# Rotary turns of twelve query tiles: block transfers and a column of signs for products with a constant matrix

## The chip, the cores and the metric

One core of one Trainium2 chip runs the whole program once. The metric is the device time of one execution in microseconds, as the median of several runs.

## The reference, cut to what matters

The model is two blocks one after the other on 512 tokens of width 1024, all float32. The first block (convolution branch, spatial gating, mixture of experts) and the feed-forward parts of the second are not touched. The part that matters is the mixing part of the second block:

```python
p = h @ w_in[l]                                  # 512 x 2416
qa, ka, va, qi, ki, wi, cq, ckv, kr = jnp.split(p, split_points, axis=-1)
qa = apply_rope(qa.reshape(B, T, 8, 64), cos_a, sin_a)     # attention queries
ka = apply_rope(ka, cos_a, sin_a)
qi = apply_rope(qi.reshape(B, T, 16, 64), cos_i, sin_i)    # index queries
ki = apply_rope(ki, cos_i, sin_i)
out_a = dsa_sparse_attention(qa, ka, va, qi, ki, wi)       # top 128 keys by index score
out_b = mla_attention(cq, ckv, kr, g_q_lat[l], g_kv_lat[l], w_uq[l], w_ukv[l], cos_b, sin_b)

def apply_rope(x, cos, sin):
    x1, x2 = jnp.split(x, 2, axis=-1)
    return jnp.concatenate([x1 * cos - x2 * sin, x1 * sin + x2 * cos], axis=-1)
```

## The kernel before

The program is written engine by engine, each with its own queue of instructions and explicit semaphores. Activations lie transposed: features on the 128 partitions, the 512 tokens along the free axis. A tile of queries is 128 x 512 and holds two heads of 64 features. The stage that the change touches is `pe_mix`, `act_mix`, `dve_mix`, `pool_mix` and `sp_mix`.

The projection `h @ w_in` runs as 20 chunks of weights in 5 groups of 4 chunks. For each chunk SyncE loads 512 KB, ScalarE writes the high half (`split_hi`, L551), VectorE the low half (`split_lo`, L556), and TensorE makes 24 products of 128x512 in three terms (L561 to L563). After four chunks VectorE reads the four banks of the group (`read_group`, L3028). Group 0 holds the keys and the narrow columns, groups 1 and 2 the eight tiles of index queries (`qi`, ropes 2 to 9), group 3 the latents, and group 4 the four tiles of attention queries (`qa`, ropes 10 to 13).

A rotation of a tile x is x * cos + R x * sin, where R is a constant 128x128 matrix that exchanges the halves of each head and negates one of them. TensorE makes R x as one float32 product of 128x512 (`rotate_rows`, L2791; the trace shows two passes for each product), GpSimd makes x * cos (L3240 for ropes 0 to 9, L3256 for 10 to 13), VectorE makes R x * sin out of PSUM (`sine`, L3045; `sines_of_queries`, L3063), and VectorE (L3053) or GpSimd (L3260) adds the two. TensorE's `rotate_rows` stands after chunk 4 (ropes 0 and 1), chunk 8 (ropes 2 to 5), chunk 12 (ropes 6 to 9), and, for ropes 10 to 13, between the K and V products of the latents (L2858, L2864) behind the last chunk.

The index products (`index_pair`, L2809) follow chunks 9, 10, 13 and 14 and read the rotated tiles; ScalarE takes their positive part, and VectorE accumulates the scores (`accumulate`, L3084). From chunk 15 on VectorE selects the top 128 keys by rounds of L3100 and L3103, in `choose_to` steps that are woven into its other work: 30 steps by the end of chunk 19, 38 before `sines_of_queries`, 70 after it, and then the rotation of the latent queries (L3162, L3166) with six more steps. When L3166 has summed a half, SyncE copies it by four DMAs (L2728) into the place from which the first scores of the attention are made (L2747). `hold_clock` (L426) makes products that nothing reads, to keep TensorE busy.

GpSimd's queue also carries `term_step` (L2260): DMAs of 704 KB each that prepare weight sums in DRAM for a later stage. 7 stand before its rotations, 7 behind the cosine of rope 5, 8 behind that of rope 9, 5 behind the latent squares.

Of the kernel before, what the change touches and what calls it, by code (L numbers as in the profile page):

```python
# [52 lines left out]
ALU = mybir.AluOpType  # L53
# [50 lines left out]
K_HALF = 1220  # L104
K_CA = 1224
# [7 lines left out]
def constants():  # L113
# [21 lines left out]
    c[:, K_HALF] = p // CAP  # L135

# [16 lines left out]
def program(nc, A, out):  # L153
    with ExitStack() as ctx:
# [2482 lines left out]
        sine_of_query = [after_groups[:, 3584 + T * i:4096 + T * i] for i in range(4)]  # L2637

# [4 lines left out]
        rot_bank = [4, 5] + [0, 1, 2, 3] + [4, 5, 6, 7] + [4, 5, 6, 7]  # L2643
# [140 lines left out]
        def pe_mix(pe):  # L2784
# [14 lines left out]
            def index_pair(p):  # L2799
                q, b = idx_pairs[p]  # L2800
                S = P * (b + 1)
                if b == 3:
                    pe.wait_ge(mx["rope"], R_QI + q + 1)
                    pe.wait_ge(mx["rot_read"], R_QI + (4 if q < 4 else 8))
# [20 lines left out]
            for c in range(4, 4 * N_MIX):  # L2825
# [15 lines left out]
                if c == 8:  # L2841
                    rotate_rows(range(2, 6))
                if c == 12:
                    rotate_rows(range(6, 10))
# [15 lines left out]
            rotate_rows(range(R_QA, len(ropes)))  # L2860
# [7 lines left out]
            pe.wait_ge(mx["rot_read"], len(ropes))  # L2868
# [41 lines left out]
        def act_mix(act):  # L2910
# [43 lines left out]
            for c in range(4, 20):  # L2954
                if c + 2 < 20:
                    mix_hi(c + 2)
                else:
                    split_hi(act, C_MO, c - 18)
# [9 lines left out]

            act.wait_ge(mx["acc"], 2 * N_IDX)
# [52 lines left out]
        def dve_mix(dve):  # L3022
# [16 lines left out]
            split_lo(dve, C_MIX, 5)  # L3039
            def sine(r):  # L3040
                kind = ropes[r][1]
                dve.wait_ge(mx["rot"], r + 1)
                if r >= 3:
                    dve.wait_ge(mx["rope"], r - 2)
                dve.tensor_tensor(pr[:, r % 3, :], psum[:, rot_bank[r], :], sin_of[kind], ALU.mult).then_inc(  # L3045
                    mx["rot_read"], 1)

            def rotated(r):
# [3 lines left out]
                if r:  # L3052
                    dve.tensor_tensor(src, cos_at(r), pr[:, r % 3, :], ALU.add).then_inc(mx["rope"], 1)  # L3053
                    return
# [5 lines left out]
            def sines_of_queries():  # L3060
                for r in range(R_QA, len(ropes)):
                    dve.wait_ge(mx["rot"], r + 1)
                    dve.tensor_tensor(sine_of_query[r - R_QA], psum[:, rot_bank[r], :], sin_of["A"], ALU.mult).then_inc(  # L3063
                        mx["rot_read"], 1)
# [67 lines left out]
            for c in range(3, 20):  # L3132
# [5 lines left out]
                if c % 4 == 3:  # L3138
                    read_group(c // 4)
# [85 lines left out]
        def pool_mix(pool):  # L3225
# [28 lines left out]
            for r in range(R_QA, len(ropes)):  # L3254
                pool.wait_ge(mx["rot"], r + 1)
# [137 lines left out]
```

## Time and profile before

| | |
|---|---|
| Median of 3 runs | 1966.82 us (1966.52 to 1968.87) |
| The profiled execution | 1966.62 us |
| Its span in the trace | 1964.6 us, 26526 instructions |
| TensorE busy | 1880.4 us (96%) |
| VectorE, ScalarE, GpSimd busy | 1110.6, 673.7 and 354.2 us (57%, 34%, 18%) |
| Granted TensorE clock, mean | 0.997 |

The mixing stage up to the start of its attention lies at about 1305 to 1489 us of the span. Rows of the page and of the trace have times in us from the start of the span. A group of instructions is named by its line, engine, operation, tile written <- tiles read, sizes and count.

### The profile page before, as it was taken

What the parts mean: (1) busy time and instruction counts of PE and PEld (TensorE: products, weight loads), DVE (VectorE), ACT (ScalarE), POOL (GpSimd) and SP (SyncE); (2) the same over time, 40 slices, a digit from 0 to 9 for tenths busy, and PEclk for the clock granted to TensorE, in tenths of its full rate; (3) what the DMA queues carried; (4) which work ended last, traced back from release to release, by engine and by line L of the source; (5) the groups of instructions that cost most, each with busy time, mean ns of one, the idle gap of its engine ahead of it and who ended that gap; (6) DMA issues with size and microseconds to landing.
All of it is one profiled execution on the core that took longest, in us unless ns stands there. A gap on an engine that the chain in (4) does not pass through costs nothing. (4 is left out here: it accounts for less than half of the span.)

```text
span 1964.6 us, 26526 instructions
## 1 busy us (share of the span) xinstructions
PE 1880.4 (96%) x9569; PEld 1343.8 (68%) x9570; DVE 1110.6 (57%) x1680; ACT 673.7 (34%) x1030; POOL 354.2 (18%) x430
## 2 busy tenths in 40 slices
PE   8999999998997789998899999999999899999998
PEld 7888888785332233333588887887665589999886
DVE  4998993444111111111634336965687638777897
ACT  4234435432000000000422224562336746444566
POOL 2023233201221112222011000012255500010100
PEclk9999999999999999999999999999999999999999
DMA  6489999997999999999466534677980065666565
GB/s 208 149 291 291 252 326 237 301 381 290 424 426 427 426 427 425 393 426 423 163 214 214 155 96 140 193 181 184 234 192 12 1 148 155 181 181 183 174 197 171
DMA packets 202680, 485.84 MB, mean 247 GB/s; under 512 B 34892, under 2 KB 113153, under 8 KB 177370
## 3 DMA queue, kind: packets, MB, share of 16 engines
q1 hardware_dynamic: 171802, 384.24, 54.5%
q0 software_dynamic: 30768, 100.31, 20.0%
q8 instruction: 62, 1.02, 0.2%
q14 instruction: 32, 0.26, 0.0%
q10 hardware_dynamic: 16, 0.00, 0.0%
HBM read 475.17 MB, written 111.67 MB: 299 GB/s over the span
## 5 line engine op out<-in xcount | busy, mean ns | idle before, releaser
L561 PE MATMUL psum<-h_hi,w_hi 128*128 128x512 f32 (+1 forms) x1240 | 449.8, 363 | 6.2 <-DVE h_lo L1043 1.9
L563 PE MATMUL psum<-h_hi,w_lo 128*128 128x512 f32 (+1 forms) x1240 | 445.3, 359 | 0.0
L562 PE MATMUL psum<-h_lo,w_hi 128*128 128x512 f32 (+1 forms) x1240 | 445.1, 359 | 0.0
L556 DVE TENSOR_TENSOR w_lo<-w_raw,w_hi 128x1024 fp32r<-128x1024 f32 (+1 forms) x144 | 178.2, 1238 | 296.3 <-ACT w_hi L551 296.2
L551 ACT ACTIVATE w_hi<-w_raw 128x1024 fp32r<-128x1024 f32 (+1 forms) x144 | 151.7, 1053 | 502.0 <-PE psum L563 454.3
L561 PEld LDWEIGHTS psum<-h_hi,w_hi 128*128 128x128 f32 x1240 | 234.2, 189 | 46.0 <-issue 7.1
L562 PEld LDWEIGHTS psum<-h_lo,w_hi 128*128 128x128 f32 x1240 | 234.3, 189 | 35.3 <-issue 1.4
L563 PEld LDWEIGHTS psum<-h_hi,w_lo 128*128 128x128 f32 x1240 | 234.2, 189 | 34.9
L1409 PE MATMUL psum<-arena,w_raw 128*64 128x512 f32 x800 | 181.7, 596 | 13.5 <-DMA arena<-in_w_expert_up_dram 12.6
L1544 ACT ACTIVATE w_raw<-psum 128x256 f32<-128x256 f32 x36 | 13.8, 384 | 464.1 <-PE psum L1409 464.1
L1071 DVE SCALAR_TENSOR_TENSOR arena<-arena,vec 128x512 f32<-128x512 f32 x240 | 162.6, 748 | 1.0 <-ACT arena L898 1.0
L1409 PEld LDWEIGHTS psum<-arena,w_raw 128*64 128x64 f32 x800 | 54.5, 137 | 118.1 <-issue 95.7
L2044 ACT ACTIVATE w_hi<-w_raw 128x1024 fp32r<-128x1024 f32 x77 | 81.7, 1061 | 115.9 <-PE psum L563 114.8
L2092 DVE TENSOR_TENSOR w_lo<-w_raw,w_hi 128x1024 fp32r<-128x1024 f32 x77 | 95.6, 1242 | 43.5 <-ACT w_hi L2044 43.4
L1419 PE MATMUL psum<-arena,w_raw 128*64 128x512 f32 x400 | 93.0, 608 | 12.7 <-DMA arena<-in_w_expert_down_dram 11.7
L1788 POOL DMA_INDIRECT expert_rows<-w_raw,scatter_now x34 | 35.1, 1032 | 330.8 <-DVE w_raw L1713 322.1
L1702 DVE TENSOR_TENSOR w_raw<-w_raw,psum 128x256 f32<-128x256 f32 x36 | 15.2, 421 | 138.2 <-ACT w_raw L1544 138.2
L2260 POOL DMA_DIRECT2D weight_terms<-in_w_down_dram x72 | 58.8, 896 | 188.8 <-DMA weight_terms<-in_w_down_dram 108.0
L1713 DVE TENSOR_SCALAR w_raw<-psum,arena 128x512 f32<-128x512 f32 x34 | 25.5, 751 | 118.3 <-PE psum L1419 118.3
L2346 PE MATMUL psum<-w_hi,down_operands 128*128 128x512 f32 x224 | 87.7, 391 | 1.9 <-DVE down_operands L2587 1.9
L2348 PE MATMUL psum<-w_lo,down_operands 128*128 128x512 f32 x224 | 87.2, 389 | 0.0
L2347 PE MATMUL psum<-w_hi,down_operands 128*128 128x512 f32 x224 | 87.2, 389 | 0.0
(394 smaller groups left out, 3197.8 us busy)
## 6 DMA issues: line engine op xcount, KB each, us to landing
arena<-in_w_expert_gate_dram SPq DMA_DIRECT2D x44, 1024.0 KB, 19.4
arena<-in_w_expert_up_dram SPq DMA_DIRECT2D x44, 1024.0 KB, 23.4
arena<-in_w_expert_down_dram SPq DMA_DIRECT2D x22, 2048.0 KB, 28.8
weight_terms<-in_w_down_dram POOLq DMA_DIRECT2D x60, 512.0 KB, 7.9
w_raw<-in_w_in_dram SPq DMA_DIRECT2D x44, 512.0 KB, 8.6
expert_down_third<-in_w_expert_down_dram SPq DMA_DIRECT2D x10, 2048.0 KB
expert_input<-in_w_expert_gate_dram SPq DMA_DIRECT2D x20, 1024.0 KB, 22.4
expert_input<-in_w_expert_up_dram SPq DMA_DIRECT2D x20, 1024.0 KB, 26.3
```

The lines of the kernel that those rows point to most:

```text
L551: eng.activation(whi[:, (c0 + k) % SPLIT, :, 0:n], raw[:, slot, :, 0:n], ACT.Copy).then_inc(w_hi, 1)
L556: eng.tensor_tensor(wlo[:, s, :, 0:n], raw[:, slot, :, 0:n], whi[:, s, :, 0:n].bitcast(F32), ALU.subtract).then_inc(w_lo, 1)
L561: eng.matmul(o, w_h, x_h, start=first, stop=False)
L562: eng.matmul(o, w_h, x_l, start=False, stop=False)
L563: return eng.matmul(o, w_l, x_h, start=False, stop=last)
L1071: dve.scalar_tensor_tensor(out=conv[:, c, :], in0=a_pad[:, c, j:j + T], scalar=conv_w[:, c, j:j + 1], in1=conv[:, c, :], op0=ALU.mult, op1 ...
L1409: mm = pe.matmul(psum[q * CAP:(q + 1) * CAP, 2 + b, :].rearrange("p (w n) -> p w n", w=2), xgT[b][:, k % 4, (k // 4) * CAP:(k // 4 + 1) * ...
L1419: mm = pe.matmul(psum[q * CAP:(q + 1) * CAP, 6 + b, :], heT[b][:, k % 2, (k // 2) * CAP:(k // 2 + 1) * CAP], wd[w][:, k, q * T:(q + 1) * T ...
L2092: dve.tensor_tensor(wlo4[:, r % SPLIT], raw4[:, r % RAW], whi4[:, r % SPLIT].bitcast(F32), ALU.subtract).then_inc(w_lo, 1)
L2346: pe.matmul(o, x_h[:, a, f], w_h[:, a, :], start=begin, stop=False)
L2347: pe.matmul(o, x_l[:, a, f], w_h[:, a, :], start=False, stop=False)
L2348: mm = pe.matmul(o, x_h[:, a, f], w_l[:, a, :], start=False, stop=end)
```

## The change

For the eight index tiles and the four attention tiles the product with R is gone. ScalarE issues four DMAs for each group of four tiles (`turn_rows`), which copy blocks of 32 partitions x 2048 floats from the tiles to another place with neighbouring blocks exchanged: 0 with 1, 2 with 3. The sign of R becomes a column of constants (`K_SIGN`, -1 or 1 by partition), and VectorE makes (copy * sign) * sin in one `scalar_tensor_tensor` (`signed_sine`), in place, from two SBUF tiles. Groups 1 and 2 use the place of the attention queries (`ar3[:, 0:2048]`), which the last group read fills later; group 4 uses the place where the four sines stood before. Ropes 0 and 1 stay as they were. TensorE no longer waits for the sines to be read before its index products and before the latent queries' products; it waits for the last group read instead.

```diff
+K_SIGN = 1221
+    c[:, K_SIGN] = np.where(p % HDA < HDA // 2, -1, 1)
+        turned_keys = [qa[:, i, :] for i in range(4)]
+        rows_at = [ar3[:, 18688:20736], ar3[:, 20736:22784], ar3[:, 0:2048]]
+        turn_in = x_in[0:3]
+
+        def turn_rows(act_eng, i):
+
+            group_read(act_eng, G_MIX + (1, 2, 4)[i])
+            if i == 1:
+                act_eng.wait_ge(mx["rope"], R_QI + 4)
+            to, source = rows_at[2] if i < 2 else after_groups[:, 3584:5632], rows_at[i]
+            for b in (32, 0, 96, 64):
+                act_eng.dma_start(to[b:b + 32], source[b ^ 32:(b ^ 32) + 32]).then_inc(turn_in[i], 16)
...
-                    pe.wait_ge(mx["rot_read"], R_QI + (4 if q < 4 else 8))
...
-                if c == 8:
-                    rotate_rows(range(2, 6))
-                if c == 12:
-                    rotate_rows(range(6, 10))
...
-            rotate_rows(range(R_QA, len(ropes)))
...
-            pe.wait_ge(mx["rot_read"], len(ropes))
+            group_read(pe, G_MIX + 4)
...
             for c in range(4, 20):
+                if c in (8, 12):
+                    turn_rows(act, c // 4 - 2)
                 if c + 2 < 20:
                     mix_hi(c + 2)
...
+            turn_rows(act, 2)
             act.wait_ge(mx["acc"], 2 * N_IDX)
...
+            def signed_sine(r, part):
+                dve.wait_ge(turn_in[(r - R_QI) // 4], 80)
+                dve.scalar_tensor_tensor(out=part, in0=part, scalar=sign, in1=sin_of["A"], op0=ALU.mult,
+                                         op1=ALU.mult).then_inc(mx["rot_read"], 1)
+
             def sine(r):
                 kind = ropes[r][1]
+                if r >= R_QI:
+                    signed_sine(r, turned_keys[(r - R_QI) % 4])
+                    return
...
-                    dve.tensor_tensor(src, cos_at(r), pr[:, r % 3, :], ALU.add).then_inc(mx["rope"], 1)
+                    part = turned_keys[(r - R_QI) % 4] if r >= R_QI else pr[:, r % 3, :]
+                    dve.tensor_tensor(src, cos_at(r), part, ALU.add).then_inc(mx["rope"], 1)
...
             def sines_of_queries():
                 for r in range(R_QA, len(ropes)):
-                    dve.wait_ge(mx["rot"], r + 1)
-                    dve.tensor_tensor(sine_of_query[r - R_QA], psum[:, rot_bank[r], :], sin_of["A"], ALU.mult).then_inc(
-                        mx["rot_read"], 1)
+                    signed_sine(r, sine_of_query[r - R_QA])
...
                 if c % 4 == 3:
+                    if c == 19:
+                        dve.wait_ge(mx["rope"], R_QA)
                     read_group(c // 4)
...
             for r in range(R_QA, len(ropes)):
-                pool.wait_ge(mx["rot"], r + 1)
+                pool.wait_ge(turn_in[2], 80)
                 pool.tensor_tensor(cos_at(r), ropes[r][0], cos_of[ropes[r][1]], ALU.mult).then_inc(mx["cos"], 1)
```

The semaphores `turn_in` are at 16 from the loads of x at the start, so 80 means that all four transfers of a group have landed.

## Rows read from the trace of the kernel before

**Rows 1.** The page, part 1: busy time, share of the span and instructions of each engine.

```profile
PE 1880.4 (96%) x9569; PEld 1343.8 (68%) x9570; DVE 1110.6 (57%) x1680; ACT 673.7 (34%) x1030; POOL 354.2 (18%) x430
```

**Rows 2.** Timeline of TensorE, two stretches: start, us, line, tiles, count.

```profile
1356.96 3.60 PE L2791 MATMUL psum<-arena,const 128*128 128x512 f32 x8
...
1360.63 0.39 PE L562 MATMUL psum<-h_lo,w_hi 128*128 128x512 f32 x1
...
1365.97 1.45 PE L2809 MATMUL psum<-arena 64*128 64x512 f32 x6
...
1394.60 3.60 PE L2791 MATMUL psum<-arena,const 128*128 128x512 f32 x8
```

**Rows 3.** The same before the attention, with idle time and its releaser.

```profile
1462.41 7.03 PE L2864 MATMUL psum<-arena 128*128 128x512 f32 x16
...
1486.44 1.46 PE L426 MATMUL psum<-const 128*128 128x256 f32 x6
1489.15 0.68 PE L2747 MATMUL psum<-arena 96*128 96x128 f32 x4 [1.25 <-DMA arena<-expert_input]
```

**Rows 4.** Stretches: each engine's busy us, clock, DMA share, GB/s.

```profile
1460.00:1480.00 20.00, 20.00 (x47) 8.77 (x47) 20.00 (x59) 5.15 (x9) 11.19 (x9) 1.00 0.18 62
```

**Rows 5.** Timeline of VectorE, 1454 to 1485.

```profile
1454.99 2.28 DVE L3028 TENSOR_TENSOR arena<-psum,stat_std 128x2048 f32<-128x2048 f32 x1
...
1463.91 2.46 DVE L3063 TENSOR_TENSOR expert_input<-psum,const 128x512 f32<-128x512 f32 x4
...
1484.20 0.67 DVE L3166 TENSOR_TENSOR expert_input<-expert_input 128x512 f32<-128x512 f32 x1
```

**Rows 6.** One line, SyncE's DMAs of 64 KB: duration of issue, then landing.

```profile
L2728 SPq DMA_DIRECT2D arena<-expert_input x8: 588/591/740, 1484.9 to 1489.5; - x8
...
DMA to landing us min/median/max: 2.0/2.0/2.3
```

**Rows 7.** DMA issues at 1342, 1400 and 1340 to 1500: KB each, us to landing.

```profile
w_raw<-in_w_in_dram SPq DMA_DIRECT2D x1, 512.0 KB, 3.5
...
w_raw<-in_w_in_dram SPq DMA_DIRECT2D x3, 512.0 KB, 5.7
...
up_terms<-up_terms POOLq DMA_DIRECT2D x11, 704.0 KB, 14.0
```

**Rows 8.** Stretches where the transfers will fall, columns as in rows 4.

```profile
1356.00:1359.00 3.00, 3.00 (x10) 1.71 (x10) 0.98 (x2) 1.06 (x1) 2.63 (x3) 1.00 0.34 118
1393.00:1396.00 3.00, 3.00 (x12) 1.99 (x11) 0.98 (x2) 1.06 (x1) 1.97 (x2) 1.00 0.81 159
...
1458.00:1461.00 3.00, 3.00 (x8) 1.33 (x7) 3.00 (x11) 1.83 (x4) 0.85 (x1) 1.00 0.99 251
```

**Rows 9.** Timeline of VectorE around the rotations of groups 1 and 2.

```profile
1354.01 2.28 DVE L3028 TENSOR_TENSOR arena<-psum,stat_std 128x2048 f32<-128x2048 f32 x1
1358.31 1.65 DVE L556 TENSOR_TENSOR w_lo<-w_raw,w_hi 128x1024 fp32r<-128x1024 f32 x1 [2.02 <-ACT w_hi L551]
...
1362.28 1.46 DVE L3053 TENSOR_TENSOR arena<-arena 128x512 f32<-128x512 f32 x1
...
1391.67 2.28 DVE L3028 TENSOR_TENSOR arena<-psum,stat_std 128x2048 f32<-128x2048 f32 x1
```

**Rows 10.** The page, part 5: a group of instructions of the first block.

```profile
L1071 DVE SCALAR_TENSOR_TENSOR arena<-arena,vec 128x512 f32<-128x512 f32 x240 | 162.6, 748 | 1.0 <-ACT arena L898 1.0
```

**Rows 11.** Timeline of GpSimd at groups 1 and 3.

```profile
1356.37 4.74 POOL L3240 TENSOR_TENSOR arena<-arena,const 128x512 f32<-128x512 f32 x3 [22.00 <-DVE arena L3028]
1361.90 1.29 POOL L3240 TENSOR_TENSOR arena<-arena,const 128x512 f32<-128x512 f32 x1 [0.80 <-DVE arena L3053]
...
1460.15 4.96 POOL L3256 TENSOR_TENSOR arena<-arena,const 128x512 f32<-128x512 f32 x4 [2.93 <-PE psum L2791]
```

**Rows 12.** Stretches in the expert stage, columns as in rows 4.

```profile
700.00:706.00 6.00, 2.13 (x14) 0.78 (x11) 1.02 (x2) 0.38 (x1) 0.00 (x0) 0.99 1.02 428
706.00:710.00 4.00, 4.00 (x14) 1.25 (x12) 0.00 (x0) 0.00 (x0) 0.00 (x0) 0.59 1.01 426
```

More of the change, by code:

```diff
@@ L2642, in program @@
         pe_rows = slice(NOPE, HQ)
-        rot_bank = [4, 5] + [0, 1, 2, 3] + [4, 5, 6, 7] + [4, 5, 6, 7]
+        rot_bank = [4, 5]
         rot_group = [0] * 2 + [1] * 4 + [2] * 4 + [4] * 4
@@ L3039, in dve_mix @@
             split_lo(dve, C_MIX, 5)
+            sign = const[:, K_SIGN:K_SIGN + 1]
+            def signed_sine(r, part):
+                dve.wait_ge(turn_in[(r - R_QI) // 4], 80)
+                dve.scalar_tensor_tensor(out=part, in0=part, scalar=sign, in1=sin_of["A"], op0=ALU.mult,
+                                         op1=ALU.mult).then_inc(mx["rot_read"], 1)
             def sine(r):
                 kind = ropes[r][1]
+                if r >= R_QI:
+                    signed_sine(r, turned_keys[(r - R_QI) % 4])
+                    return
                 dve.wait_ge(mx["rot"], r + 1)
-                if r >= 3:
-                    dve.wait_ge(mx["rope"], r - 2)
                 dve.tensor_tensor(pr[:, r % 3, :], psum[:, rot_bank[r], :], sin_of[kind], ALU.mult).then_inc(
```

## The prediction

> **What bounds the kernel now.** I read the page first: TensorE is busy 96% of 1964.6 us [rows 1], and the granted clock is 1.00 in every stretch of this stage that I quote [rows 4, 8]. That average says nothing of the stage in question, so I went on to the timelines of 1350 to 1490 us, engine by engine. The twelve rotations removed are three groups of four, and the groups don't have the same bound.
>
> Groups 1 and 2 (eight index-query tiles) stand in TensorE's stream without a gap on either side [rows 2]. VectorE and ScalarE idle there, waiting for TensorE. What TensorE saves is saved, if nothing new makes it wait. Group 3 (four attention-query tiles) also stands in a full TensorE stream [rows 3], but there VectorE is busy 20.00 of 20.00 us [rows 4], TensorE ends first and then idles 1.25 us for a DMA [rows 3]. That DMA (eight copies of the rotated latent queries) is released by VectorE's L3166, at the end of its unbroken chain: group read, sines, selection steps, L3162, L3166 [rows 5]. So before the attention stage VectorE is the bound, and time saved on TensorE there is worth nothing.
>
> **Removed from TensorE.** In [rows 2] the eight passes start at 1356.96; the second matmul after them starts at 1360.63, where it would have started 0.23 us after 1356.96 (the spacing of the stream). 1360.63 - 1356.96 - 0.23 = 3.44 us for four rotations, 0.86 each. Groups 1 and 2 are worth at most 6.9 us, group 3's 3.44 us is off the path.
>
> **Added: the transfers.** Each group becomes four DMAs of 32 partitions x 8 KB, 256 KB each, 1 MB in all, issued by ScalarE once VectorE's group read is done. The consumers wait for all four. No row shows a transfer of this form. An issue of 32 partitions costs 0.59 us, and 64 KB land 2.0 us after it [rows 6]; a 512 KB load lands in 3.5 us on a quiet stretch and in 5.7 us on a crowded one [rows 7]. So 1 MB takes at least 2.0 + 2 x 1.5 = 5.0 us from the first issue. At the crowded rate it is 2.0 + 2 x 3.7 = 9.4 us. On GpSimd's software queue, which fills the engines from 1363 on, 704 KB need 14.0 us [rows 7]; that is my other end. I choose by how full the 16 DMA engines are at the place [rows 8]: 6.0 us for group 1 (share 0.34), 7.5 us for group 2 (0.81 to 1.00; what is queued is mostly small packets, which I expect to lose against rows of 8 KB), 8.0 us for group 3 (0.99, that queue still draining).
>
> Apart from that, the Trainium skill (SBUF — State Buffer, Door 1: The DMA port swizzle) says that 32 partitions reach only 8 of 16 ports and gives 189 GB/s for 1 MiB. That estimate would be 5.5 + 2 = 7.5 us for each group, would leave 0.1 us of gain in groups 1 and 2 each, would make group 3's wait 1.0 us, and the end 1973.9 us. No row here shows it.
>
> **Group 1.** The group read ends at 1356.29 [rows 9], so the first issue is at 1356.4 and the last byte lands at 1362.4. VectorE then needs two sines and one sum before the first index product: 2 x 0.68 (the SCALAR_TENSOR_TENSOR of two SBUF inputs, L1071, 162.6 us for 240 [rows 10]) + 0.60 = 1.96, so 1364.4. TensorE's chunk 9 took 5.57 us (1360.40 to 1365.97 [rows 2]); starting at 1356.96 it ends at 1362.5. TensorE waits 1.9 us; of 3.44 remain 1.5. With 5.0 us to landing 2.5 remain.
>
> ScalarE also stands behind the four issues (2.4 us). Its next work, the high half of chunk 10, moves from 1357.2 to 1358.9, VectorE's low half to about 1361; both are due when chunk 10 starts, after 1368, so this costs nothing. The fourth cosine on GpSimd waits for a sum, so the software DMAs queued behind it start some 2 us later.
>
> **Group 2.** The same, 37.6 us later: read ends 1393.95 [rows 9], landing 1394.0 + 7.5 = 1401.5, first sum 1403.5, TensorE due at 1394.60 + 5.57 = 1400.2. It waits 3.3 us, 0.1 remains. With 5.0 us to landing 2.6 remain, with 14 us it loses 6.4. Groups 1 and 2 together: 1.6 us gained, between -4.9 and +5.1.
>
> **Group 3.** The group read ends at 1457.27 [rows 5]; landing at 1457.4 + 8.0 = 1465.4. VectorE reaches its four sines at 1463.91 [rows 5] and now waits 1.5 us (0 to 7.5), with its whole chain queued behind it. Then the sines themselves. They read PSUM and one SBUF tile today, and the four take 2.46 us while GpSimd's cosines L3256 run at the same time [rows 5, 11]. The new ones have two SBUF inputs. Where such an instruction meets a GpSimd TENSOR_TENSOR, [rows 9] show blocking: L556 at 1358.31 takes 1.65 us where 1024 elements take 1.23 at the rate of L3063 [rows 5], L3053 at 1362.28 takes 1.46 where 512 elements take 0.62, and ends 0.55 us after the GpSimd instruction of 1361.90, and three GpSimd instructions take 4.74 us where three of the later four take 3.72 [rows 11]. So they take turns. Group 3's cosines and sines are now released by the same semaphore: 4 x 0.68 + 3 x 1.24 = 6.4 us if VectorE goes first, 7.7 if GpSimd does, against 2.4 us now. I take the middle, +4.7 us. The chain before attention becomes 1.5 + 4.7 = 6.2 us longer.
>
> ScalarE's issues stand before its copies of the K products, so the first copy starts at 1459.8. The V products wait for two of them (1.2 us) and start at 1460.9 instead of 1462.41 [rows 3]: TensorE keeps 1.5 of its 3.44 us and only comes earlier to its wait.
>
> The other edits cost nothing: the waits dropped or added against sums (TensorE's on the eight sines, VectorE's before the last group read, ScalarE's before group 2's transfers) are on events over 10 us old when they are reached.
>
> **The clock.** TensorE would end at 1487.9 - 1.5 = 1486.4 and start attention at 1489.15 + 6.2 = 1495.4: 9 us idle. In [rows 12] it idles 3.87 of 6 us and the granted clock of the 4 us behind that is 0.59, so at the 1.2 GHz level for most of them: 4 x 0.41 = 1.6 us of TensorE time lost. I add 1.6 us.
>
> **The sum.** 1966.6 (the profiled execution, 1964.6 + 2.0 around it) - 1.6 + 6.2 + 1.6 = 1972.8. The median of three is 0.2 higher, so 1973.0 us.
>
> **Rivals.** About 0.2% (3.9 us) is what a measurement can tell from no change: above 1970.7 is slower, under 1962.9 faster.
>
> (1) The shared port costs VectorE one GpSimd instruction instead of three or four, because VectorE's queue issues its sines back to back. Then 1.5 + 1.2 = 2.7 us is added to the chain, the idle is still over 5 us, and the end is 1966.8 - 1.6 + 2.7 + 1.6 = 1969.5. For it: the trace shows only single meetings, never four in a row. The Trainium skill (SBUF — State Buffer, Who interferes with whom) calls the port an exclusive lock that whoever issues first holds for a whole instruction; by that rule this rival falls, and the single meetings in the trace agree with it (0.42 and 0.84 us of blocking).
>
> (2) Faster: the transfers land in 5.0 us at all three places and rival 1 holds too. Groups 1 and 2 gain 5.1, the chain loses 1.2 at most: 1966.8 - 5.1 + 0.6 = 1962.3, without a clock loss since the idle stays near 3.4 us. It decides from a landing within 5.2 us of the first issue. For it: ScalarE's queue is its own and nearly empty. Against: the share is 0.81 and 0.99 in two of three places [rows 8].
>
> (3) Crowded: 11 us to landing in groups 2 and 3. Group 2 loses 3.4 instead of gaining 0.1, group 3 waits 4.5 instead of 1.5, and TensorE's 6.8 us idle in group 2 costs another 1.6 of clock. 1973.0 + 3.5 + 3.0 + 1.6 = 1981.1.
>
> **How the numbers follow.** Forecast 0.45, rival 1 0.25, rival 2 0.13, rival 3 0.17. The forecast's own range, with landing 1 us off either way and either engine first at the port, is 1970 to 1976. Slower: most of the forecast and rival 3, 0.57. Same: rival 1 and the edges, 0.30. Faster: 0.13. The range leaves about one in ten on each side: 1962.5 to 1980.
>
> **What would show each step.** Landing times of the twelve transfers (6.0, 7.5, 8.0 us). TensorE's idle before L2809 at both groups, put down to the sum on VectorE (1.9 and 3.3 us). VectorE's idle before the query sines, and their duration together (6.4 to 7.7 us). TensorE's idle before the first score (near 9 us) and a granted clock near 0.5 right after it. If the twelve sines take 0.75 us each and VectorE idles under 1 us before the last four, the forecast is wrong on the fast side; if a transfer takes over 10 us, on the slow side.

## The result, and the profile after

| | before | changed |
|---|---|---|
| Median | 1966.97 us (1965.43 to 1968.87, 6 runs) | 1982.92 us (1979.06 to 1988.83, 6 runs) |
| Span of the profiled execution | 1964.6 us | 1982.3 us |
| Granted TensorE clock, mean | 0.997 | 0.988 |

The ratio is 1.0083 [1.0067, 1.0099]: slower, as forecast, but by 16 us where 6 were forecast, and outside the range. The page of the changed kernel shows as good as nothing of it; the busy times are those of [rows 1] within 4 us:

```profile
PE 1882.5 (95%) x9545; PEld 1347.3 (68%) x9546; DVE 1113.2 (56%) x1680; ACT 673.9 (34%) x1030; POOL 354.8 (18%) x430
```

VectorE's timeline of the changed kernel has the landmarks. L3039 is the group read (before: L3028), L3055 the new signed sine, L3186 the first sum of the latent queries (before: L3166). The first number is the start and the second the duration, in us; the bracket is idle time and what ended it.

```profile
1355.19 2.28 DVE L3039 TENSOR_TENSOR arena<-psum,stat_std 128x2048 f32<-128x2048 f32 x1
...
1364.42 1.42 DVE L3055 SCALAR_TENSOR_TENSOR arena<-arena,const 128x512 f32<-128x512 f32 x2 [1.29 <-DMA arena<-arena]
...
1393.41 2.28 DVE L3039 TENSOR_TENSOR arena<-psum,stat_std 128x2048 f32<-128x2048 f32 x1
...
1406.16 1.42 DVE L3055 SCALAR_TENSOR_TENSOR arena<-arena,const 128x512 f32<-128x512 f32 x2 [4.73 <-DMA arena<-arena]
...
1461.38 2.28 DVE L3039 TENSOR_TENSOR arena<-psum,stat_std 128x2048 f32<-128x2048 f32 x1
...
1475.50 5.77 DVE L3055 SCALAR_TENSOR_TENSOR expert_input<-expert_input,const 128x512 f32<-128x512 f32 x4 [5.12 <-DMA expert_input<-arena]
...
1499.10 0.67 DVE L3186 TENSOR_TENSOR expert_input<-expert_input 128x512 f32<-128x512 f32 x1
```

The same landmarks of before are in [rows 5, 9]: reads at 1354.01, 1391.67 and 1454.99, the sum at 1484.20. The lag of the changed kernel at the four is 1.18, 1.74, 6.39 and 14.90 us, and at the end 17.7. The first 1.18 us lie ahead of the change (over the kernels of this study the first of these reads starts anywhere from 1352.9 to 1356.6). So group 1 cost +0.56 us, group 2 +4.65, group 3 +8.51, and the rest after that about +2.8. (The two profiled executions are 17.7 us apart, the medians 16.0; the six times of the changed kernel spread over 9.8 us.)

ScalarE's queue, the issues of the three groups' transfers:

```profile
1357.51 3.20 ACTq L2651 DMA_DIRECT2D arena<-arena  x4
1395.73 3.26 ACTq L2651 DMA_DIRECT2D arena<-arena  x4
1463.70 2.46 ACTq L2651 DMA_DIRECT2D expert_input<-arena  x4
```

From first issue to landing (the start of L3055 behind its wait) that is 6.9, 10.4 and 11.8 us. TensorE's timeline shows what they cost there; L2822 are the index products (before: L2809), L2761 the first score:

```profile
1366.49 3.93 PE L2822 MATMUL psum<-arena 64*128 64x512 f32 x12 [2.75 <-DVE arena L3073]
...
1373.67 0.50 PE L563 MATMUL psum<-h_hi,w_hi 128*128 128x512 f32 x1
...
1408.23 6.78 PE L2822 MATMUL psum<-arena 64*128 64x512 f32 x20 [6.29 <-DVE arena L3073]
1415.50 0.70 PE L2822 MATMUL psum<-arena 64*128 64x256 f32 x4 [0.49 <-ACT arena L2947]
1416.13 0.50 PE L563 MATMUL psum<-h_hi,w_hi 128*128 128x512 f32 x1
...
1503.89 1.19 PE L2761 MATMUL psum<-arena 96*128 96x128 f32 x4 [10.78 <-DMA arena<-expert_input]
```

Each of these idle times is followed by products that run slowly. In stretches of the changed kernel that hold the idle time and what follows (busy us of each engine, granted clock, DMA share, GB/s; the last stretch lies behind the first scores):

```profile
1362.00:1370.00 8.00, 5.25 (x18) 2.59 (x18) 6.71 (x9) 2.25 (x3) 3.42 (x4) 0.79 0.39 97
1406.00:1414.00 8.00, 5.77 (x16) 2.57 (x18) 7.84 (x10) 2.43 (x3) 5.56 (x5) 0.57 1.01 264
1496.00:1508.00 12.00, 4.11 (x12) 3.51 (x13) 8.06 (x26) 1.52 (x6) 0.55 (x1) 0.50 0.19 46
1508.00:1512.00 4.00, 4.00 (x13) 2.55 (x12) 2.77 (x12) 1.25 (x4) 1.61 (x4) 0.82 0.00 0
```

The same 24 index products take 5.96 us at the clock of 1.00: in the kernel before the row of L2809 at 1365.97 is followed by the next chunk at 1371.93,

```profile
1371.93 0.50 PE L561 MATMUL psum<-h_hi,w_hi 128*128 128x512 f32 x1
```

and now they take 7.18 us (1366.49 to 1373.67) and 7.90 us (1408.23 to 1416.13). So group 1 is 3.44 saved, less 2.75 idle, less 1.2 of clock: -0.5, where the landmarks say -0.56. Group 2 is 3.44 - 6.29 - 1.9 = -4.8, landmarks -4.65. Group 3 is 5.12 us of waiting plus sines of 5.77 instead of 2.46: 8.43, landmarks 8.51. From the first score to the end of the span are 478.4 us against 475.45 before (1964.6 - 1489.15): 3.0 us. The clock is at 0.50, its lower level, for the first 4 us of scores and at 0.82 in the next 4; 4 x 0.50 + 4 x 0.18 = 2.7 us of that is the clock.

The length of the idle time does not decide what the clock does. The run of the experiments in which SyncE's w_in loads come first is the same kernel up to this place, idles the same 2.75 us in group 1, and makes its index products at full speed:

```profile
1365.89 1.77 PE L2822 MATMUL psum<-arena 64*128 64x512 f32 x8 [2.75 <-DVE arena L3073]
```

From the first group read to the second are 37.66 us in the kernel before, 38.22 in the changed one, 37.0 in this run and 39.1 with group 1 alone: with nearly the same idle time, group 1 comes out between 0.7 us gained and 1.4 us lost, by the clock.

### The profile page after: what moved, and what is told of

Read it like the earlier page. It is cut to its first block and busy times, and to the rows that moved or that the text cites. A ratio compares the mean times of both kernels' runs of the same rounds, so it can differ in the third digit from the quotient of the medians.

```text
span 1982.3 us, 26484 instructions
## 1 busy us (share of the span) xinstructions
PE 1882.5 (95%) x9545; PEld 1347.3 (68%) x9546; DVE 1113.2 (56%) x1680; ACT 673.9 (34%) x1030; POOL 354.8 (18%) x430
## 5 line engine op out<-in xcount | busy, mean ns | idle before, releaser
L2262 POOL DMA_DIRECT2D weight_terms<-in_w_down_dram x72 | 58.8, 896 | 198.2 <-DMA weight_terms<-in_w_down_dram 111.3
L1715 DVE TENSOR_SCALAR w_raw<-psum,arena 128x512 f32<-128x512 f32 x34 | 25.5, 751 | 117.7 <-PE psum L1421 117.7
```

## The experiments

Every run has the kernel before on the same chip beside it. Line numbers are each kernel's own. "Group n alone" keeps the others on products with R.

**One group at a time** (`BY_DMA` is `(1,)` and `(2,)` in the other two; what follows from it in the queues is left out).

```diff
+        BY_DMA = (0,)
+        def by_dma(r):
+            return r >= R_QI and (r - R_QI) // 4 in BY_DMA
```

> Only group 1 (ropes 2 to 5) turns by transfers; the others by products as before. Theory A (each group's cost is its own, as read off the changed kernel's trace): four transfers land 6.9 us after the first issue, TensorE idles 2.8 us before the first index product, and the slower clock behind it takes what is left of the 3.4 us saved: 1966 to 1969 us. Theory B (the cost is in the late transfers pushing all later DMA traffic back): group 1 alone already makes the end late through the queues behind it, 1970 or more.

> Only group 2 (ropes 6 to 9) turns by transfers. Theory A: landing 9 to 10.5 us after the first issue, idle 5 to 6.5 us before the index product, a clock of 0.5 for some us behind it: +4 to +5 us, 1971 to 1972. Theory B (group 2 is crowded only because group 1's transfers and the later start of the software DMAs pushed the queues back): landing 7 to 8 us, idle under 3.5 us, +1 or less, 1967 to 1968.

> Only group 3 (ropes 10 to 13) turns by transfers. Theory A: landing near 11.8 us after the first issue, VectorE waits 5 us for it, the four sines take 5.8 us, TensorE idles over 10 us before attention: +10 to +12 us, 1977 to 1979. Theory B (the backlog comes from groups 1 and 2): landing 8 to 9 us, VectorE waits 1.5 to 2.5 us, +7 or less, up to 1974.

Group 2 alone: 1971.0 us (1.0020 [1.0011, 1.0030]), landing 10.7 us after the first issue, TensorE idle 6.54 us. Group 3 alone: 1977.1 us (1.0048 [1.0031, 1.0064]), landing 11.3 us, VectorE idle 4.65 us, sines again 5.77 us. Both are as theory A says to within half a microsecond, and neither needs the others' delay.

Group 1 alone was a surprise: 1989.8 us (1.0115 [1.0099, 1.0132]), slower than all three groups together. The landing (6.9 us) and TensorE's idle time (2.71 us) were those of theory A; the time was theory B's, late through the queues behind. Its stretch 1420 to 1440 shows an idle TensorE, ScalarE's timeline what it waited for, and the DMA page of 1405 to 1440 who had the engines (queue, packets, MB, share; then issues with KB and us to landing):

```profile
1420.00:1440.00 20.00, 0.65 (x4) 0.50 (x4) 1.58 (x2) 2.67 (x3) 1.64 (x2) 0.57 1.02 252
```

```profile
1437.33 1.06 ACT L553 ACTIVATE w_hi<-w_raw 128x1024 fp32r<-128x1024 f32 x1 [25.30 <-DMA w_raw<-in_w_in_dram]
```

```profile
q0 software_dynamic: 1143, 5.72, 80.8%
q1 hardware_dynamic: 2106, 2.32, 21.0%
...
w_raw<-in_w_in_dram SPq DMA_DIRECT2D x3, 512.0 KB, 30.1
```

SyncE had issued those loads from 1403.42 on, GpSimd its passes of gradient terms (L2262) from 1402.53. In the kernel before it is the other way round, 1398.96 against 1400.80:

```profile
1398.96 1.04 SPq L538 DMA_DIRECT2D w_raw<-in_w_in_dram  x1
```

```profile
1400.80 1.69 POOL L2260 DMA_DIRECT2D up_terms<-in_w_up_dram  x2
```

The first of the four loads, issued at 1403.42, shows the delay best:

```profile
w_raw<-in_w_in_dram SPq DMA_DIRECT2D x1, 512.0 KB, 33.9
```

The four landed 33.9, 34.2, 30.1 and 22.9 us after their issue. In the kernel before, two were issued well ahead of the passes and landed in 5.4 and 5.7 us; the third, issued 0.24 us ahead of them, took 12.4 us and the fourth, 5.3 us behind their start, 15.6. My reading: w_in loads issued behind the first software transfers are held up by them, the more of the four the worse. The last part below tests it.

**The shared port.** GpSimd's four cosines wait until VectorE's four sines are done.

```diff
-                pool.wait_ge(turn_in[2], 80)
+                pool.wait_ge(mx["rot_read"], len(ropes))
```

> The changed kernel, but GpSimd's cosines of group 3 wait until VectorE's four sines are done, so the two never read the shared port together. Theory A (the port): the four sines fall from 5.8 to 2.8 us and the whole is 3 us faster than the changed kernel, 1979 to 1981. Rival: the sines are slow because both operands are in SBUF or because the transfers write beside them: they stay near 5.8 us and the time stays at 1983.

1980.6 us (1.0067 [1.0051, 1.0084]), 2.3 under the changed kernel. The intervals of the two overlap, so the time alone would not show it; the rows do. VectorE's row:

```profile
1474.38 2.74 DVE L3055 SCALAR_TENSOR_TENSOR expert_input<-expert_input,const 128x512 f32<-128x512 f32 x4 [5.04 <-DMA expert_input<-arena]
```

The four take 2.74 us alone and 5.77 beside the cosines, so 3.0 us of group 3 are the meeting with GpSimd. The wait before them did not change (5.04 us). One by one (shortest, median and longest in ns) the sines and cosines of the changed kernel are

```profile
L3055 DVE SCALAR_TENSOR_TENSOR expert_input<-expert_input,const x4: 752/1749/1753, 1475.5 to 1479.5; 128x512 f32<-128x512 f32 x4
L3276 POOL TENSOR_TENSOR arena<-arena,const x4: 1708/1714/1767, 1475.6 to 1480.7; 128x512 f32<-128x512 f32 x4
```

The first sine goes free in 0.75 us, the other three take 1.75 and start 1.68 us apart, with a cosine starting between any two: three meetings, at 1.0 us each. This agrees with the exclusive lock of the Trainium skill (SBUF — State Buffer, Who interferes with whom), but each meeting cost 1.0 us and not the 1.24 us of a whole cosine.

**The clock.** TensorE makes products that nobody reads while it waits for turned tiles, so that the granted clock should stay up; the short fill has 7, 15 and 28 for 8, 20 and 36.

```diff
+                if c in {9: 8, 13: 20}:
+                    group_read(pe, G_MIX + (1 if c == 9 else 2))
+                    hold_clock(pe, 0 if c == 9 else 4, {9: 8, 13: 20}[c])
-            hold_clock(pe, 4, 3)
+            hold_clock(pe, 4, 36)
```

> The changed kernel with products that nothing reads filled into TensorE's three waits (8 before the first index product of group 1, 20 in group 2, 36 instead of 3 before the attention), so that it hardly idles. Theory A (a part of the loss is the slower clock behind the idle): granted clock near 1.00 after all three waits, and 4 to 5 us faster than the changed kernel, 1978 to 1979. Rival (the wait is all, the low clock falls into waiting time): under 1.5 us faster, 1981.5 or more.

> The changed kernel with TensorE kept busy by constant products while it waits for the turned tiles, as in the run that took 1982.8 us, but the fill is cut to what that trace shows: in group 2 it ran 2.2 us past the sum it should only cover and before attention 3.8 us past the first rotary part of the queries (fills now 7 and 15 products of 0.44 us, and 28 before attention). Theory A (the clock gives 1.6 us in each of groups 1 and 2 and 2.9 at attention's start once the fill does not overshoot, and the filled run only lost them again to its own length): 1980.2 - 2.2 - 3.8 = 1974.2 us by span, 1974.8 by time (1973.5 to 1977). Theory B (the clock is no cause; the time follows the waits alone): 1980.5 to 1983.5 us, as the changed kernel.

The long fill took 1982.8 us (1.0085 [1.0068, 1.0102]), no gain. Its clock was 1.00 in every 20 us stretch from 1355 to 1535, but the fill was too long: before attention it ran to 1504.67, 3.8 us past the moment at which the first score could start (L3189 at 1496.09 plus the 4.79 us that lie between sum and score in the changed kernel). The short fill took 1979.0 us (1.0063 [1.0047, 1.0080]), 4.0 under the changed kernel; these intervals overlap too, and the rows have to carry it. Its TensorE row:

```profile
1489.49 12.25 PE L428 MATMUL psum<-const 128*128 128x256 f32 x56
1501.58 0.68 PE L2761 MATMUL psum<-arena 96*128 96x128 f32 x4
```

From first score to end are 475.6 us (1977.2 - 1501.58) against 478.4 in the changed kernel and 475.45 before: the clock cost 2.8 us there. Theory A's direction held, its 1974.8 did not: in group 2 the transfers, issued at 1394.12, landed only at 1405.88, 11.8 us, so that 1.13 of the 2.2 us cut from the fill came back as idle time behind it.

**What the landing is made of.** First the width: four transfers of all 128 partitions and 512 floats of each, the same bytes. They exchange nothing, so the output is not the rotated one; the run is for its landings alone.

```diff
-            for b in (32, 0, 96, 64):
-                act_eng.dma_start(to[b:b + 32], source[b ^ 32:(b ^ 32) + 32]).then_inc(turn_in[i], 16)
+            for b in range(4):
+                act_eng.dma_start(to[:, T * b:T * b + T], source[:, T * b:T * b + T]).then_inc(turn_in[i], 16)
```

> The changed kernel, but each group's four transfers copy all 128 partitions by 512 columns (256 KB each as before) and exchange nothing, so the output is not the rotated one. Theory A (32 partitions move at half the rate of 128: 205 GB/s with 93% of the DMA engines in the changed kernel's trace, against 350 GB/s for loads of 128 partitions): group 1 lands in about 5 us instead of 6.9, at over 300 GB/s. Rival (copies within the SBUF are slow whatever their form): 6.5 to 7 us, near 205 GB/s.

1977.6 us in one run. Landings: at most 4.8 us in group 1 (VectorE did not wait), 7.7 in group 2, 11.8 in group 3. With 4.8 us group 1 gained: 34.96 us from the first group read to the second, where the kernel before takes 37.66. The packets of the turning queue q10 in group 1, here (1357.3 to 1362) and, under it, in group 2 of the kernel with no software transfers (next paragraph; 1394 to 1400.8):

```profile
q10 hardware_dynamic: 576, 1.05, 57.7%
```

```profile
q10 hardware_dynamic: 192, 1.05, 67.6%
```

57.7% of 4.7 us are 2.7 us of all 16 engines for 1.05 MB; 67.6% of 6.8 us are 4.6 us, 1.7 times as much for the same bytes. I put this down to the number of partitions, but the edit also cuts the rows from 8 KB to 2 KB and drops the exchange between partitions, and no run keeps these apart. At its densest the changed kernel moves the blocks of 32 partitions at 205 GB/s, with 93% of the engines' time (1359.5 to 1361.5):

```profile
DMA packets 77, 0.41 MB, mean 205 GB/s; under 512 B 27, under 2 KB 27, under 8 KB 27
...
q10 hardware_dynamic: 77, 0.41, 92.9%
```

Then the queues. All later gradient passes leave the stage (`STEPS_IN_MIX = {0: 7}`):

> The changed kernel, with the last 20 of GpSimd's weight-sum DMAs moved from the rotations of the mixing stage to behind the attention. Theory A (groups 2 and 3 wait in the DMA engines behind that software queue): the transfers of all three groups land 6 to 7 us after their first issue (10.4 and 11.8 in the changed kernel), idle at group 2 near 2.8 us, VectorE's wait at group 3 under 1 us. Rival (SyncE's many small packets hold them up): group 2 still lands in 9 us or more. The end time says little, since the moved DMAs meet later loads.

2025.7 us in one run. The passes, done later, fall into other work: from 1600 to 1700 us TensorE is busy for 52 us, in the changed kernel for 99. I did not follow that further. Read for its landings, 6.9, 6.8 and 10.5 us, theory A held in group 2 and failed in group 3 (VectorE still idle for 3.81 us). SyncE's small rows had also passed before group 2 in this kernel (q1 has 157 packets and 15.6% in its 6.8 us), so 6.8 us is group 2 free of both, and both together make 3.6 of its 10.4 us. (The landing of group 2 is not steady: it is 9.9 to 11.8 us over the runs with the same transfers and the same queues, and group 3's is 11.3 to 11.8.) What has the engines in the changed kernel, at 1395.7 to 1398 (q1 is SyncE, q0 software, ScalarE's q10 has nothing yet) and at 1400 to 1406:

```profile
q1 hardware_dynamic: 1236, 0.26, 56.1%
q0 software_dynamic: 57, 0.24, 50.6%
```

```profile
q10 hardware_dynamic: 145, 0.74, 54.2%
q1 hardware_dynamic: 2161, 0.41, 46.7%
```

2161 packets of under 512 bytes keep 46.7% of the engines beside ScalarE's rows of 8 KB. They do not lose against them.

Group 3 in the kernel without software transfers, first 2 us of its stretch (1456 to 1458): SyncE's loads have all engines.

```profile
q1 hardware_dynamic: 372, 0.59, 106.7%
```

The order of issue (32, 96, 0, 64 in place of 32, 0, 96, 64):

> The changed kernel with the four blocks of a group issued in the order 32, 96, 0, 64 instead of 32, 0, 96, 64, so that neighbours in the queue touch different halves of the partitions. Theory A (a transfer is bound by itself, they follow each other): nothing changes, 1981 to 1985, group 1 lands in 6.9 us. Rival (two transfers to the same half block each other): group 1 lands in 5 to 5.5 us, 2 to 4 us faster.

1981.3 us (1.0073 [1.0056, 1.0090]), landings 6.6, 11.1, 11.4 us: as theory A says, it matters little.

SyncE's two constant loads issued after group 3 has landed, and SyncE's w_in loads issued ahead of the small w_uq and w_ukv loads:

```diff
                         sp.wait_ge(w_used, C_MIX + 20)
+                        sp.wait_ge(turn_in[2], 80)
```

```diff
+            for k in range(4):
+                load_chunk(sp, C_MIX + 16 + k, (C_MIX + k) % RAW, wv[:, 2 * k:2 * k + 2, C_QA:C_QA + CN])
             sp.wait_ge(w_used, C_MIX)
             wuq = A["w_uq_2"].rearrange("o (k p) (h f) -> (o k) p h f", p=P, f=HQ)
...
-            for k in range(4):
-                load_chunk(sp, C_MIX + 16 + k, (C_MIX + k) % RAW, wv[:, 2 * k:2 * k + 2, C_QA:C_QA + CN])
```

> The changed kernel in which SyncE issues its two constant loads (64 KB in 512-byte rows and 512 KB) after the turned tiles of group 3 have landed, not 1.8 us before their transfers are issued. Theory A (group 3 lands in 11.8 us instead of 7 because SyncE's loads and GpSimd's software transfers stand ahead of it in the 16 engines; without the constants it is 1.5 to 3 us less): landing of group 3 in 9 to 10.3 us, VectorE idle before its signed sines 2 to 3.6 us instead of 5.1, time 1980.5 us. Theory B (the rows of 2 KB written to other partitions are what is slow): landing 11.3 to 12.3 us as in the changed kernel and no gain.

> The changed kernel with SyncE's w_in loads ahead of the w_uq and w_ukv loads. Theory A (group 2's landing of 10.4 us is made by the software transfers and by whatever SyncE has queued; rows of 2 to 4 KB take the place of rows of 256 to 512 bytes and the bytes stay): landing 9 to 11 us, group 3 unchanged, time 1982.9 us within 2.5 us. Theory B (the small rows hold the engines and the turned tiles wait for them): landing of group 2 falls to 7 to 8 us as with no software transfers beside it, and the time to 1979 us.

With the constants late: 1984.0 us in one run, landing 11.2 us, VectorE idle 4.49 us. At most 0.6 us came from the constants, which is no more than the landing varies; theory A wanted 1.5 to 3, and its size fell. With the loads first the landing of group 2 stayed at 10.5 us. That does not show that small rows are as cheap as large ones: over the landing the small rows of the changed kernel (0.98 MB) hold 55.1% of the engines, 5.7 us, and the 1.08 MB of SyncE's that took their place 36.0%, 3.7 us, while the software transfers rose from 11.3% to 25.5%. So what the small rows alone cost the landing stays open. The time was 2003.5 us (1.0178 [1.0161, 1.0195]) because SyncE's w_out loads now stood behind the small ones, the first issued at 1465.79, not at 1424.30, and ScalarE waited for it:

```profile
1471.60 1.06 ACT L553 ACTIVATE w_hi<-w_raw 128x1024 fp32r<-128x1024 f32 x1 [26.64 <-DMA w_raw<-in_w_out_dram]
```

TensorE had 2.65 us of work in 1460 to 1480.

Last, who holds the engines while group 3 lands in the changed kernel (1463.7 to 1475.5):

```profile
q0 software_dynamic: 194, 0.91, 37.9%
q1 hardware_dynamic: 633, 1.19, 36.0%
q10 hardware_dynamic: 192, 1.05, 28.9%
```

They are full for the whole 11.8 us: 4.5 us for software transfers, 4.2 for SyncE, 3.4 for the turning transfers. With the full width it is 4.7, 4.5 and 2.7 us (1457.3 to 1469.1), full again, so the 9.2 us of the other two queues decide and the saving of the width does not show.

**Group 1 alone again: who starves whom, and is there a gain to be had?** Three ways around the stall, each with the same edit of the kernel before as its control: the eight gradient passes behind rope 9 moved behind the latents; the w_in loads first, as above; and GpSimd waiting before the eight passes until the first of the w_in loads is split.

```diff
-STEPS_IN_MIX = {0: 7, 6: 7, 10: 8, 13: 5}
+STEPS_IN_MIX = {0: 7, 6: 7, 13: 13}
```

```diff
             def some_steps(after):
+                if after == 10:
+                    pool.wait_ge(w_lo, C_MIX + 17)
```

In three of the group 1 kernels the index products also come a chunk later, so that TensorE has a chunk to work on while the transfers land:

```diff
-        idx_after = {9: (0, 1), 10: (2, 3), 13: (4, 5), 14: (6, 7)}
+        idx_after = {10: (0, 1, 2), 11: (3,), 13: (4, 5), 14: (6, 7)}
```

> Group 1 alone turned by transfers, as in the run that took 1989.8 us, but the eight passes of the gradient terms that GpSimd runs after rope 9 (L2262, transfers by software descriptors) are moved behind its sums of the latents. Theory A (the 20 us of that run were w_in loads issued 0.9 us after the eight software transfers began and starved behind them, landing 30 us late): with the passes moved, the loads land in 3 to 6 us as in the kernel before, TensorE has no stretch of 20 us with 0.65 us of work, and the time is 1967.5 us (1966 to 1969.5: turning group 1 by transfers cost +0.55 in the changed kernel). Theory B (the stall comes from the turning transfers' delay of VectorE or ScalarE, whatever the software transfers do): the stall near 1420 to 1441 stays and the time is above 1985 us.

> The kernel before, all turns by products, with the same move of the eight gradient passes: the control of the run beside it. Theory A (the passes' place matters only where it meets a load): 1966.8 us, within 0.2% of the kernel before (1964.5 to 1968.5). Theory B (the passes steal something wherever they run, and later in the stage they cost or free more): outside 1963 to 1971 us.

> Group 1 alone turned by transfers, the gradient passes moved as in the first run of this set, and the index products of tiles 0 to 3 a chunk later (three tiles behind chunk 10, one behind chunk 11, in place of two behind 9 and two behind 10), so that TensorE has a chunk of 8 us to work on while the transfers land in 6.9 us. Theory A (TensorE's products are 3.44 us of path in a group of four and the landing is then covered): 3.44 + 0.55 us less than the first run of this set, less up to 1.5 us for the last eviction of scores before chunk 12: 1964.3 us (1962.5 to 1966.5). Theory B (VectorE's sums of the scores move along and hold the split of the next chunks or the sums of group 2, which takes the gain back): 1966.5 to 1971 us.

> Group 1 alone turned by transfers, index products of tiles 0 to 3 a chunk later (three tiles behind chunk 10, one behind 11), the gradient passes at their old place behind rope 9; and SyncE issues the four w_in loads of chunks 16 to 19 ahead of the small w_uq and w_ukv loads, not behind them. Theory A (what starved was a w_in load issued after the software transfers had begun; issued ahead of them it lands in about 3 us; and the later index products cover the landing, as the 2 us gained in the run with the passes moved): no stall of TensorE near 1420, GpSimd's latents and cosines on time, 1964.5 us (1962 to 1967). Theory B (the small loads, now behind the software transfers, are starved instead and arrive late for the products of the latents, or hold SyncE's w_out loads): above 1968 us.

> The kernel before, all turns by products, with SyncE's w_in loads ahead of the w_uq and w_ukv loads: the control of the run beside it. Theory A: nothing waited for these loads before, so 1966.8 us within 0.2% (1963 to 1970.7). Theory B: above 1968, for the same reason as in the run beside it.

> Group 1 alone turned by transfers, index products of tiles 0 to 3 a chunk later, everything else at its old place; GpSimd waits before the eight gradient passes behind rope 9 until the first of SyncE's four w_in loads has landed and been split (so all four have been issued ahead of the software transfers). Theory A (what cost 20 us in group 1 alone was only that order): no stall of TensorE in 1400 to 1480, the passes start near 1408 to 1412 and have been issued before the squares of the latents come near 1434, and the gain of 1.2 to 1.8 us that the two pairs with controls showed is left: 1965.2 us (1963.5 to 1967.5). Theory B (the passes, begun about 10 us later, hold GpSimd's sums of the latents or starve SyncE's w_out loads near 1420): 1972 us or more.

> The kernel before, all turns by products, with the same wait of GpSimd ahead of the eight gradient passes: the control of the run beside it. Theory A: 1966.8 us within 0.2% (1963 to 1970.7), and the run beside it 1 to 2 us under it. Theory B: as much above 1968 us as the run beside it.

| edit beside | group 1 by transfers | all by products (control) |
|---|---|---|
| passes moved | 1985.3 us, 1.0098 [1.0081, 1.0114] | 1984.7 us, 1.0090 [1.0074, 1.0107] |
| passes moved, index later | 1983.6 us, 1.0079 [1.0063, 1.0096] | the same control |
| loads first, index later | 1983.2 us, 1.0078 [1.0061, 1.0095] | 1985.0 us, 1.0089 [1.0072, 1.0106] |
| GpSimd waits, index later | 1974.1 us, 1.0032 [1.0021, 1.0043] | 1975.2 us, 1.0042 [1.0025, 1.0059] |

All my absolute times were missed, and the controls say why: the three detours cost the kernel with all turns by products as much as the one with transfers. With the passes moved, the 25 us wait for w_in is gone, but GpSimd drives software transfers until 1484 and its copies of the rotary key, at 1451.72 in the kernel before, come some 30 us later; in the control VectorE's first sum of the latent queries waits 13.91 us for GpSimd. First the control's row, then the kernel before:

```profile
1484.21 4.50 POOL L3252 COPY arena<-arena 32x512 f32<-32x512 f32 x8
```

```profile
1451.72 5.50 POOL L3252 COPY arena<-arena 32x512 f32<-32x512 f32 x8
```

With the loads first, SyncE's w_out loads come some 22 us late (issued from 1440.21 and, in the control, from 1439.66; 1417.74 in the kernel before). The wait of GpSimd is the smallest detour: the passes begin at 1416.65 and the w_in loads, issued from 1404.60 on and so ahead of them, land in 4.4 to 7.3 us (median 6.0) where they took 22.9 to 34.2:

```profile
1416.65 1.69 POOL L2262 DMA_DIRECT2D up_terms<-in_w_up_dram  x2 [17.41 <-DVE w_lo L558]
```

```profile
w_raw<-in_w_in_dram SPq DMA_DIRECT2D x4, 512.0 KB, 6.0
```

No stall of 20 us is left, here or in the other detours near 1420, so the meeting of the two queues is shown as its cause. (The wait keeps them 12 us apart; how near they may come was not tried.) Its 7 us over the kernel before are the sums of the latents, which start 6.5 us late behind the passes (1439.33 against 1432.83), leave TensorE idle for 6.17 us (4.51 in the control) and delay the last group read by about 7 us in this kernel and its control alike (1462.64 and 1462.09, [rows 5] 1454.99).

The gain that the change had in it is best read between two landmarks, VectorE's first group read and its read of the latents. That stretch takes 75.3 to 75.4 us in the kernel before and in all three controls, 74.7 with the passes moved and the index products at their old place (its clock stayed at 1.00), and 72.6 in all three kernels with the index products a chunk later (1355.31 to 1427.93 in the last of them). So 2.7 of the 3.44 us are real when the landing is covered. At the end 1.1 to 1.8 us of it are left against the controls, in each pair inside or at the edge of the spread. No kernel of this study beats the kernel before.

## Why the prediction was right and wrong

**Right: the bounds.** Groups 1 and 2 are on TensorE's path and group 3 on VectorE's. TensorE's saving of 3.44 us in groups 1 and 2 adds up with idle time and clock to within 0.15 us of the landmarks. The sum for a short landing holds too: 2.5 us were to remain of 3.44 with a landing in 5.0 us, and with the full width group 1 landed in 4.8 and kept 2.7.

**Right in kind, too large: the sines of group 3.** Forecast 6.4 to 7.7 us instead of 2.4 by the single meetings at the port; measured 5.77, under that range, with 3.0 us of it gone when the two engines are kept apart. VectorE goes first and is held up three times, as forecast; a meeting costs 1.0 us and not 1.24. Rival 1 (one GpSimd instruction only) is out. The term was +4.7 and is +3.3.

**Wrong: the landings.** This is the step that failed. The three terms were 6.0, 7.5 and 8.0 us and measured 6.9, 10.4 and 11.8. Two steps under them failed, and a row was read too kindly. The slope of 3.5 to 5.7 us for 512 KB came from loads that reach all partitions; blocks of 32 partitions move at 205 GB/s and take 1.7 times the engines' time (width, row length and exchange not kept apart). The Trainium skill (SBUF — State Buffer, Door 1: The DMA port swizzle) has 189 GB/s for this; I had it in the text and put it aside because no row showed it. My estimate from it of 7.5 us without competition is close to the 6.9 and 6.8 us seen, in part by luck: the figure is for one transfer of 1 MiB with its fixed part in it, and my 2 us on top count that part again; without them it is 5.5 us. The other step is "mostly small packets, which I expect to lose against rows of 8 KB": they keep 46.7% of the engines. The row is the 5.7 us of [rows 7], my crowded stretch: it is the median of three loads, which took 5.4, 5.7 and 12.4 us, and the fourth, issued 4 us behind that row's stretch, took 15.6. In group 3 I added 0.5 us to group 2's term for a queue that was still draining; the other two queues held the engines for 8.7 of the 11.8 us. Rival 3 with its 11 us in groups 2 and 3 is what came, and its 1981.1 is 1.8 us under the measured median. I gave it 0.17. Its number is near by errors that offset each other: it has group 1 gaining 1.5 us (lost 0.56), the sines at +4.7 (+3.3) and 1.6 us of clock at the attention (3.0).

**Wrong: the clock.** I charged it once, 1.6 us, where TensorE idles for 9 us. It fell after all three waits, also behind 2.75 us of idle in group 1, and cost 1.2, 1.9 and 3.0 us. The 1.6 came from a row of 4 us; at attention's start the clock was at 0.50 for 4 us, with TensorE busy in all of them, and at 0.82 for the next 4. Why it stayed low longer there, and why the same 2.75 us left it alone in two other kernels, is open.

**The sum.** Forecast -1.6 + 6.2 + 1.6 = 6.2. Measured +0.56 + 4.65 + 8.5 + 3.0 = 16.7, to which the profiled pair adds 1.2 us of entry (17.9 against the 17.7 of the spans). Of the difference the landings are 7.5 us (idle times 2.75, 6.29 and 5.12 where 1.9, 3.3 and 1.5 were forecast), the clock is 4.5, and the sines give 1.4 back.

**Missed: the neighbour.** I wrote that the software transfers behind the fourth cosine start some 2 us later and left it there. Their order against SyncE's w_in loads is worth over 20 us (with group 1 alone 97.9 us from the first group read to that of the latents, 75.3 in the kernel before). In the changed kernel it happened to come out well (loads from 1408.95, passes from 1410.5); with group 1 alone it did not.

**Open.** Of group 3's 11.8 us about 7 are its own, if it behaves as groups 1 and 2 do alone. Taking the software transfers away gives 1.3 (10.5 without them), SyncE's constants at most 0.6. The shares say who holds the engines, but not what removing one queue gives, since the others then move up; in the kernel without software transfers SyncE's queue holds the engines for the first 2 us, and its w_out load was not tried apart.

## What to carry to other kernels

Before a product is replaced by a transfer, ask what the consumer does during the landing: here group 1's transfers gained 2.7 us of the stage with the consumer a chunk later, and with it at the old place anything from 0.7 gained to 1.4 lost; group 2's lost 4.7. Price a transfer between partitions by a transfer of the same form and by all that stands in the engines' queues, however small its packets. And compare an edit with a control that has the same detour: beside the kernel before, four runs looked like losses of 6 to 18 us for the transfers, and their controls were 7 to 18 us slow without any.

## What I had not expected of the hardware

- A 512 KB load of a hardware queue, issued 0.9 us behind the first of the software transfers, landed in 33.9 us; four issued ahead of them, in 4.4 to 7.3.
- 2161 packets of under 512 bytes (0.41 MB) held 46.7% of the 16 engines in 6 us, beside 0.74 MB in rows of 8 KB with 54.2%.
- The granted clock was 0.79 over the 8 us that hold a TensorE idle time of 2.75 us and the products behind it in the changed kernel. With group 1 alone and the passes moved, the same idle time of 2.75 us left it at 1.00 (index products in 5.96 us), so that length alone does not decide it.
- Four VectorE instructions with two SBUF inputs and four of GpSimd, released together, alternate: 0.75 us for VectorE's first, 1.75 for each of the others, 1.71 to 1.77 for GpSimd's, which took 1.27 beside sines that read PSUM.
- The issue of one of the turning transfers took ScalarE 0.51 to 1.31 us.
